# Turning the operand of the last projection earlier, and moving first logits, waits and a layer norm beside the matmuls

## The chip, the cores and the metric

One core of a Trainium2 chip runs one program. The metric is device time of one execution in microseconds; lower is better. The time before is 1919.98 us, the median of 3 runs (1919.78 to 1924.84).

## The reference

The function maps a (1, 512, 1024) f32 array through two transformer blocks, all in f32. Here is what the change touches:

```python
# first block, end of its mixer
y_attn = window_attention(q, k, v, attn_sink[l], rel_bias_table) @ w_attn_out[l]
mixed = (g_ssd * y_ssd + g_attn * y_attn) @ w_o[l]
# second block, gMLP mixer: v is (512, 2048)
v = layer_norm(jax.nn.gelu(v), ln_g, ln_b)
# second block, sliding-window attention: 16 query heads of 64, 4 key heads
logits = einsum('btkgd,bskd->bkgts', qb, kb) + alibi      # q already scaled by 1/8
m = maximum(max(logits, -1), sink); p = exp(logits - m)
o = einsum('bkgts,bskd->btkgd', p, vb) / (sum(p, -1) + exp(sink - m))
y = (o * silu(z)) @ w_out
x = x + rms_norm(y, post_g)
```

The result must hold f32 accuracy, so every large matmul is done in three passes over a high and a low part of each operand (hi*hi, hi*lo, lo*hi).

## The kernel before, in words

All engine programs are written out by hand and meet through counting semaphores; there is no planner. The 66 weight panels (1024 rows, 512 columns) stream through one buffer `raw`, `w_hi`, `w_lo` of eight tiles k. SP loads a quarter of `raw` when the low parts of the same quarter of the panel before are made (`load_quarter`, line 1045). ACT copies a tile to `w_hi` (`make_hi`, L253) once PE has finished step k of the panel before, and POOL subtracts it to get `w_lo` (`make_lo`, L257).

PE works through a panel in eight steps k (`main_step`, L294), each of 4 banks m and 3 passes, so 12 matmuls of 512 columns. Four PSUM banks `main` hold the output; the other four, `aux`, hold turned tiles, attention logits and values. The first step of a panel waits, bank by bank, until the panel before has been taken out of that bank (`bank_free`). `tail_panel` runs a panel bank by bank instead, so that rows finish one after another.

The operands of a panel that are computed in the kernel have to be turned (transposed by PE into `aux`, L366), copied to a high part (ACT, L373), and subtracted to a low part (DVE, L379). `NormOperand` counts the three as `turned`, `hi`, `ready`.

Attention (`Attention`, line 655) runs twice for each block, j = 0 and 1, 8 heads each. First comes the query panel (`query_panel`, line 1660): steps 0 to 3 for all banks, then banks 0 to 3 one at a time for the remaining steps (L1672). ACT and DVE take each finished bank as high and low queries (L713, L721). Then PE issues the logits of the first head (4 blocks c, L739 and L740; two `aux` banks in turn, so block c waits until DVE has taken block c-2), and DVE adds a bias and takes them (L780 or L782), reduces the maximum (L789), and ACT exponentiates (L806). A following panel (gates or z) has eight steps t, and in step t PE also turns the probabilities of head t-1 (L752), multiplies them with the values (L765, after ACT's copy L836) and issues the logits of head t+1. The last head, t = 7, is turned and multiplied after that panel, and by itself. ACT's tanh of z (L1494) and DVE's gating (L2114, L2116; semaphore `z_gate`) follow.

At the end of the second block all 8 tiles of the gated output `o2` are turned for the output projection P_BO, tiles 0 and 1 ahead of it, tile k+2 after step k (`turned_panel`, line 1536). The last panel is a tail panel, and the residual `res4` ends the kernel row by row (L490, L499, L521, L532, L537, L541, store L1047).

In the first block the attention output `o1` is turned one tile per step under panel P_GA+1, and `mix` for the panel P_WO: tiles 0 to 3 under P_AO+1, tiles 4 and 5 ahead of P_WO behind a wait for `ao_mul`, tiles 6 and 7 within it. DVE forms `mix` by a multiplication that frees a main bank (L2023) and an addition (L2025), bank by bank.

The gMLP's layer norm is three DVE operations on each row of 2048 columns (L2064, L2065, L2066), all before the mask of the spatial weights (L2071), which the first spatial matmul (L1749) waits for.

Of the kernel before, what the change touches and what calls it, by code (L numbers as in the profile page):

```python
# [19 lines left out]
FR = mybir.dt.float32r  # L20
# [71 lines left out]
def two_blocks(nc, d, out):  # L92
    ctx = ExitStack()
    with ctx:
# [83 lines left out]
        pt = [at("pt0", R0 + 20 * KB, [P, 384]), at("pt1", R0 + 22 * KB, [P, 384])]  # L178
        ga = at("ga", B0 + 32 * KB, [P, NT, DM])
# [291 lines left out]
        class Residual:  # L471
# [3 lines left out]
            def __init__(self, i, pan, og, gain_row, s, out_panels=2):  # L475
                self.i, self.p, self.og, self.gain_row, self.s, self.np = i, pan, og, gain_row, s, out_panels
# [4 lines left out]
            def dve_take(self, eng, n, add=False, og=None, p=None, ms=range(NT)):  # L481
                og = self.og + n if og is None else og
                p = self.p + (n + 1) * self.np - 1 if p is None else p
                for m in ms:
                    wait_full(eng, p, og, m)
                    f = fb[:, m, n * NCOL:(n + 1) * NCOL]
# [5 lines left out]
            def act_sq(self, eng, n, og=None, ms=range(NT)):  # L492
                og = self.og + n if og is None else og
                for m in ms:
# [4 lines left out]
                    eng.activation(junk_q[:, :], fb[:, m, n * NCOL:(n + 1) * NCOL], ACT.Square,  # L499
# [10 lines left out]
            def dve_gain_bank(self, eng, m, add_to=None):  # L510

                eng.wait_ge(res_sq, self.i * 2 * NT + NT + m + 1)
                eng.scalar_tensor_tensor(fb[:, m, NCOL:DM], mb[m][:, :], math.sqrt(DM), g_row[:, NCOL:DM],
                                         ALU.mult, ALU.mult).then_inc(bank_free, 1)

            def dve_gain(self, eng, ch, n, ms=range(NT)):
                eng.wait_ge(res_gain, 16 * (self.i + 1))
                for m in ms:
                    eng.wait_ge(res_sq, self.i * 2 * NT + n * NT + m + 1)
                    f = fb[:, m, n * NCOL:(n + 1) * NCOL]  # L520
# [18 lines left out]
            def dve_add_one(self, eng, m):  # L539
                eng.wait_ge(res_rs, self.i * NT + m + 1)  # L540
                eng.scalar_tensor_tensor(x_res[:, m, :], fb[:, m, :], small[:, self.s + m:self.s + m + 1], x_res[:, m, :],  # L541
# [113 lines left out]
        class Attention:  # L655
# [3 lines left out]
            def __init__(self, i, width, o, sink):  # L659
# [55 lines left out]
            def dve_take_q(self, eng, j):  # L715

                for m in range(4):
# [28 lines left out]
            def pe_turn_p(self, eng, j, t, c):  # L746
# [4 lines left out]
                for b in range(nb):  # L751
                    x = eng.transpose(self.turned_bank(t, c)[:, b * P:b * P + P], pr[t % 2][:, c, off + b * P:off + b * P + P], ident)  # L752
# [17 lines left out]
            def dve_logits(self, eng, j, t):  # L770
                for c in range(NT):
# [6 lines left out]
                    dst = lg[t % 2][:, c, off:off + nb * P]  # L778
# [7 lines left out]
            def dve_max(self, eng, ch, j, t):  # L786
                eng.wait_ge(biased, one_up(j * 32 + (self.b * 32 + t * 4 + 4)))
                mx, ng, sk = small[:, 24:28], small[:, 28 + 4 * (t % 2):32 + 4 * (t % 2)], self.sink_col(j, t)
                ch(eng.tensor_reduce(mx, lg[t % 2][:, :, 0:self.w], AX.X, ALU.max))  # L789
# [7 lines left out]
            def act_exp(self, eng, j, t, cs):  # L797
# [7 lines left out]
                for c in cs:  # L805
                    eng.activation(pr[t % 2][:, c, 0:self.w], lg[t % 2][:, c, 0:self.w], ACT.Exp,  # L806
# [49 lines left out]

            def dve_heads(self, eng, ch, j):
                self.dve_logits(eng, j, 0)
                self.dve_max(eng, ch, j, 0)
# [10 lines left out]
        att1 = Attention(0, 384, o1, "sink1")  # L870
        att2 = Attention(1, 256, o2, "sink2")
# [1389 lines left out]
```

## Time and profile before

| | before |
|---|---|
| median of 3 runs | 1919.98 us |
| profiled execution | 1920.65 us, span 1918.8 us |
| mean granted TensorE clock | 0.987 |
| PE busy | 1826.8 us (95%) |
| DVE, ACT, POOL busy | 896.3, 854.2, 862.0 us (47, 45, 45%) |
| DMA | 159.79 MB, mean 83 GB/s |
| POOL's subtraction for one `w_lo` tile (L257) | 504 times, mean 1.435 us |

The span runs from the first to the last instruction that the profile shows; the execution is 1.85 us longer. A busy engine is one with an instruction under way. An idle time of an engine is listed with its releaser, the instruction whose semaphore came last.

### The profile page before, as it was taken

To read this page: it belongs to the slowest core of one execution; us is meant where nothing else is said; L and a number is where in the kernel's file an instruction comes from. 1 tells how busy PE (TensorE), PEld (TensorE's weight loads), DVE (VectorE), ACT (ScalarE), POOL (GpSimd) and SP (SyncE) were. 2 spreads that over 40 slices of the span, in tenths; PEclk is the share of its full clock that TensorE was granted. 3 is DMA by queue.
4 is the path that set the end of the run, shared out by engine and by line. 5 is a ranking of instruction groups with operands and counts; after the bars stand their busy time and mean duration, and the time that the engine had idled before them with its cause. 6 is when DMAs were issued, how large, how long until landed. Compare 5 with 4: busy or idle time off the path is not lost.

```text
span 1918.8 us, 27606 instructions
## 1 busy us (share of the span) xinstructions
PE 1826.8 (95%) x9064; PEld 1512.2 (79%) x9064; DVE 896.3 (47%) x1311; ACT 854.2 (45%) x1796; POOL 862.0 (45%) x601
## 2 busy tenths in 40 slices
PE   8999999998999999989999999989989999999988
PEld 7787878877887878777988888867878888777766
DVE  4787888888315554234430033150261111545654
ACT  4655545554325655324442243334523332556542
POOL 4654555557353122435444444544574444531312
PEclk9999999999999999999999999999999999999989
DMA  5822211211133211422233333323222223221111
GB/s 170 145 75 67 66 55 55 65 56 55 55 110 105 72 55 50 137 77 88 88 98 99 99 92 95 109 92 128 72 93 87 88 80 108 74 83 45 55 33 56
DMA packets 46219, 159.79 MB, mean 83 GB/s; under 512 B 4763, under 2 KB 7195, under 8 KB 45884
## 3 DMA queue, kind: packets, MB, share of 16 engines
q1 hardware_dynamic: 38592, 140.53, 23.5%
q10 hardware_dynamic: 7548, 18.20, 3.8%
q8 instruction: 51, 0.84, 0.2%
q14 instruction: 28, 0.23, 0.0%
HBM read 152.42 MB, written 6.29 MB: 83 GB/s over the span
## 4 chain that ended last, share of the span: by engine, by line
PE 62%; issue 19%; DVE 9%; POOL 7%; ACT 2%; DMA 1%; DVEq 0%; ACTq 0%; POOLq 0%
PE main L294 49%; POOL w_lo L257 5%; DVE u_acc L1839 2%; PE aux L765 2%; PE main L322 2%; PE main L1672 1%; PE aux L366 1%; PE aux L1749 1%; PE aux L752 1%; PE aux L597 1%; PE aux L621 1%; DVE vv L2065 1%; DVE x_res L541 1%; PE aux L739 1%; POOL spare_lo L269 1%
## 5 line engine op out<-in xcount | busy, mean ns | idle before, releaser
L257 POOL TENSOR_TENSOR w_lo<-raw,w_hi 128x512 fp32r<-128x512 f32 x504 | 719.8, 1435 | 944.7 <-ACT w_hi L253 930.8
L253 ACT ACTIVATE w_hi<-raw 128x512 fp32r<-128x512 f32 x486 | 303.9, 630 | 700.4 <-PE main L294 687.5
L294 PE MATMUL main<-w_hi,a_hi 128*128 128x512 f32 x752 | 314.8, 419 | 2.3 <-ACT vv L1424 1.4
L294 PE MATMUL main<-w_hi,a_lo 128*128 128x512 f32 x752 | 296.9, 395 | 0.0
L294 PE MATMUL main<-w_lo,a_hi 128*128 128x512 f32 x752 | 296.0, 394 | 0.0
L294 PE MATMUL main<-a_hi,w_hi 128*128 128x512 f32 x576 | 229.6, 399 | 1.7 <-ACT u_raw L1177 1.6
L294 PE MATMUL main<-a_hi,w_lo 128*128 128x512 f32 x576 | 224.8, 390 | 0.0
L294 PE MATMUL main<-a_lo,w_hi 128*128 128x512 f32 x576 | 224.5, 390 | 0.0
L294 PEld LDWEIGHTS main<-w_hi,a_lo 128*128 128x128 f32 x752 | 142.7, 190 | 31.6
L294 PEld LDWEIGHTS main<-w_hi,a_hi 128*128 128x128 f32 x752 | 143.4, 191 | 29.7 <-issue 2.1
L294 PEld LDWEIGHTS main<-w_lo,a_hi 128*128 128x128 f32 x752 | 143.7, 191 | 23.7
L294 PE MATMUL main<-w_hi,f_hi 128*128 128x512 f32 x352 | 139.5, 396 | 6.0 <-DVE f_lo L379 6.0
L294 PE MATMUL main<-w_hi,f_lo 128*128 128x512 f32 x352 | 138.0, 392 | 0.0
L294 PE MATMUL main<-w_lo,f_hi 128*128 128x512 f32 x352 | 137.8, 391 | 0.0
L294 PEld LDWEIGHTS main<-a_hi,w_hi 128*128 128x128 f32 x576 | 108.2, 188 | 25.7 <-issue 3.0
L294 PEld LDWEIGHTS main<-a_hi,w_lo 128*128 128x128 f32 x576 | 108.1, 188 | 23.4
L294 PEld LDWEIGHTS main<-a_lo,w_hi 128*128 128x128 f32 x576 | 108.2, 188 | 22.5
L1839 DVE SCALAR_TENSOR_TENSOR u_acc<-u_raw,par,u_acc 128x510 f32<-128x510 f32 (+1 forms) x128 | 116.8, 981 | 2.4 <-DVE hst L1892 2.3
L765 PEld LDWEIGHTS aux<-v_sb,pt 128*128 128x128 f32 x544 | 70.3, 190 | 40.7 <-ACT pt L836 23.1
L765 PE MATMUL aux<-v_sb,pt 128*128 x544 | 83.7, 279 | 6.1 <-ACT pt L836 3.7
L294 PEld LDWEIGHTS main<-w_hi,f_hi 128*128 128x128 f32 x352 | 66.6, 189 | 19.6 <-DVE f_lo L379 6.2
L806 ACT ACTIVATE pr<-lg,small 128x384 f32<-128x384 f32 (+1 forms) x128 | 70.4, 552 | 24.7 <-DVE small L792 24.7
(297 smaller groups left out, 3128.9 us busy)
## 6 DMA issues: line engine op xcount, KB each, us to landing
raw<-w_stream_in SPq DMA_DIRECT2D x264, 512.0 KB, 3.5
x_res<-x_in ACTq DMA_DIRECT2D x8, 512.0 KB, 4.9
rel_rows<-rel_row ACTq DMA_DIRECT2D x1, 4096.0 KB, 44.3
bias<-rel_rows ACTq DMA_DIRECT2D x2, 1536.0 KB, 8.1
out<-x_res SPq DMA_DIRECT2D x4, 512.0 KB, 2.6
bgate<-b_gate_in ACTq DMA_DIRECT2D x4, 256.0 KB, 5.5
ln_g<-ln_g_in ACTq DMA_DIRECT2D x1, 1024.0 KB, 5.3
ln_b<-ln_b_in ACTq DMA_DIRECT2D x1, 1024.0 KB, 7.5
```

The source lines that it names most:

```text
L253: eng.activation(w_hi[:, k, :], raw[:, k, :], ACT.Copy).then_inc(hi_done, 1)
L257: eng.tensor_tensor(w_lo[:, k, :], raw[:, k, :], w_hi[:, k, :].bitcast(F32), ALU.subtract).then_inc(lo_done, 1)
L269: eng.tensor_tensor(spare.lo(k), raw[:, k, :], spare.hi(k).bitcast(F32), ALU.subtract).then_inc(lo_done, 1)
L294: mm = eng.matmul(mb[m][:, :], lhs, rhs, start=(first and k == 0 and n == 0), stop=(last and k == KT - 1 and n == 2))
L322: mm = eng.matmul(out, lhs, rhs, start=(first and k == 0 and n == 0), stop=(last and k == KT - 1 and n == 2))
L366: t = eng.transpose(b[:, m * P:m * P + P], self.src[:, m, c:c + P], ident)
L541: eng.scalar_tensor_tensor(x_res[:, m, :], fb[:, m, :], small[:, self.s + m:self.s + m + 1], x_res[:, m, :], ALU.mult, ALU.add).then_inc(r ...
L597: x = eng.matmul(ab[dr][:, :], one_row, cs_hl[:, :], start=True, stop=True)
L621: x = eng.matmul(ab[2 + i % 2][:, dr * GW:(dr + 1) * GW], b_tok[:, c, :], xw[:, dr, c, :], start=True, stop=True)
L765: x = eng.matmul(ab[3][:, c * HP:c * HP + HP], pt[c % 2][:, b * P:b * P + P], v_sb[:, lo + b, bass.ds(j * P + half * HP, HP)], start=(b == ...
L806: eng.activation(pr[t % 2][:, c, 0:self.w], lg[t % 2][:, c, 0:self.w], ACT.Exp, bias=small[:, ng + c:ng + c + 1], accum_out=small[:, sm + ...
L1839: ins = dve.scalar_tensor_tensor(acc, u_raw[:, m, i0:i0 + o1_ - o0], tap(m, k), acc, ALU.mult, ALU.add)
```

## The change

- `query_panel` calls `after(m)` behind each of its four banks. `first_logits` uses it in all four attentions: blocks 0 and 1 of the first head are issued behind bank 1, blocks 2 and 3 behind bank 2. DVE's order is that of `dve_query`.
- In block one, `o1` is turned two tiles a step in steps 0 to 3 of P_GA+1; tiles 4 and 5 of `mix` are turned behind step 1 of P_WO (with the wait for `ao_mul`), 6 and 7 behind steps 2 and 3; DVE does the four bank-freeing multiplications first and then the four additions.
- The layer norm is two operations, on 512 columns: `v_norm_cols`. The first two column blocks come before the mask, the third and fourth in the loop behind `y_lo`.
- In block two, the last head of j = 0 is issued in step 0 of the second query panel and that of j = 1 in step 0 of P_BO. Tiles 0 and 1 of `o2` are turned between steps 3 and 4 of the second query panel, 2 and 3 behind its banks 0 and 1, and 4 to 7 behind steps 2 and 3 of P_BO. The loops over j on PE, ACT and DVE are written out. Buffers: `lg2`, `pr2` (256 columns), `zt`, `fb4`, `o_hi`, `o_lo`.
- ACT makes `w_hi` tiles 0 to 2 of the last panel between its copies of the `o2` tiles 4 to 7.

```diff
+            def dve_query(self, eng, ch, j, op=None):
+                self.dve_take_q(eng, j, [0])
+                self.dve_logits(eng, j, 0, [0, 1])
+                if op is not None:
+                    op.dve(eng, [2])
+                self.dve_take_q(eng, j, [1])
+                if op is not None:
+                    op.dve(eng, [3])
+                self.dve_take_q(eng, j, [2])
+                self.dve_logits(eng, j, 0, [2, 3])
+                self.dve_max(eng, ch, j, 0)
+                self.dve_take_q(eng, j, [3])
...
+        def o_at(k):
+            return (o_hi[:, k, :], o_lo[k][:, :]) if k < 4 else (a_hi[:, k, :], a_lo[:, k, :])
+
+        op_o2 = NormOperand("op_o2", o2, [(half_k, lambda k: o_at(k)[0], lambda k: o_at(k)[1])], banks=(2, 3))
+        res4 = Residual(3, P_BO, O_BO, "b_post", 4, 1, fb4)
...
-            with act.Fori(0, 2) as j:
+            for j in range(2):
                 att2.act_take_k(act, j)
                 for k in range(4):
                     make_hi(act, j * 2 + (P_QZ + 1), k)
-                att2.act_take_q(act, j, j * 2 + P_QZ, j * 2 + O_QZ, range(3))
+                if j:
+                    op_o2.act(act, [0, 1])
+                for m in range(3):
+                    att2.act_take_q(act, j, j * 2 + P_QZ, j * 2 + O_QZ, [m])
+                    if j and m < 2:
+                        op_o2.act(act, [m + 2])
...
-            op_o2.act(act)
+            hi(P_BO + 1, [0])
+            op_o2.act(act, [4, 5])
+            hi(P_BO + 1, [1, 2])
+            op_o2.act(act, [6, 7])
             act.wait_ge(z_gate, one_up(8))
             res4.load_gain(act)
-            hi(P_BO + 1)
+            hi(P_BO + 1, range(3, KT))
...
+            def first_logits(att, j, m, og):
+                for c in {1: (0, 1), 2: (2, 3)}.get(m, ()):
+                    att.pe_logits(pe, j, 0, c, og)
...
-            panel(P_GA + 1, O_GA + 1, ao, False, aux=lambda k: op_o1.pe(pe, [k]))
+            panel(P_GA + 1, O_GA + 1, ao, False, aux=lambda k: op_o1.pe(pe, [2 * k, 2 * k + 1]) if k < 4 else None)
...
-            pe.wait_ge(ao_mul, 8)
-            op_mix.pe(pe, [4, 5])
-            panel(P_WO, O_WO, ao, False, ready=lambda k: (op_mix.ready, k + 1),
-                  aux=lambda k: op_mix.pe(pe, [k + 6]) if k < 2 else None)
+            def turn_mix_rest(k):
+                if k == 1:
+                    pe.wait_ge(ao_mul, 8)
+                    op_mix.pe(pe, [4, 5])
+                elif k in (2, 3):
+                    op_mix.pe(pe, [k + 4])
+            panel(P_WO, O_WO, ao, False, ready=lambda k: (op_mix.ready, k + 1), aux=turn_mix_rest)
...
-                        pe.wait_ge(v_norm, NT)
+                        pe.wait_ge(v_norm, j * NT + NT)
...
+            query_panel(P_QZ, O_QZ, ao, lambda m: first_logits(att2, 0, m, O_QZ))
+            heads(att2, ao, 0, P_QZ, O_QZ)
+            def turn_first_o2():
+                pe.wait_ge(z_gate, one_up(NT))
+                op_o2.pe(pe, [0, 1])
+            def under_q1(m):
+                if m < 2:
+                    op_o2.pe(pe, [m + 2])
+                first_logits(att2, 1, m, O_QZ + 2)
+            query_panel(P_QZ + 2, O_QZ + 2, ao, under_q1, under=turn_first_o2,
+                        last_head=(lambda m: att2.pe_turn_p(pe, 0, 7, m), lambda m: att2.pe_values(pe, 0, 7, m)))
+            pe.wait_ge(op_o2.ready, 4)
+            heads(att2, ao, 1, P_QZ + 2, O_QZ + 2)
+            for k in range(KT):
+                if k >= 4:
+                    pe.wait_ge(op_o2.ready, k + 1)
+                if k == 0:
+                    main_step(pe, P_BO, k, *o_at(k), False, O_BO, before=lambda m: att2.pe_turn_p(pe, 1, 7, m),
+                              after=lambda m: att2.pe_values(pe, 1, 7, m))
+                else:
+                    main_step(pe, P_BO, k, *o_at(k), False, O_BO)
+                if k == 2:
+                    pe.wait_ge(z_gate, one_up(2 * NT))
+                    op_o2.pe(pe, [4, 5])
+                elif k == 3:
+                    op_o2.pe(pe, [6, 7])
+            tail_panel(P_BO + 1, O_BO + 1, o_at)
...
+            def v_norm_cols(c0):
+                c = bass.ds(c0, NCOL)
+                for m in range(NT):
+                    part = vv[:, m, c]
+                    ch.count(dve.scalar_tensor_tensor(part, part, small[:, 16 + m:17 + m], ln_g[:, c], ALU.add, ALU.mult))
+                for m in range(NT):
+                    ch.wait(NT - 1 - m)
+                    part = vv[:, m, c]
+                    dve.scalar_tensor_tensor(part, part, small[:, 60 + m:61 + m], ln_b[:, c], ALU.mult, ALU.add).then_inc(v_norm, 1)
+            v_norm_cols(0)
+            v_norm_cols(NCOL)
...
                 y_lo(j)
+                v_norm_cols(j * NCOL + 2 * NCOL)
...
+            for j in range(2):
                 att2.dve_take_k(dve, j)
-                att2.dve_take_q(dve, j)
+                if j:
+                    op_o2.dve(dve, [0, 1])
+                att2.dve_query(dve, ch, j, op_o2 if j else None)
                 att2.dve_heads(dve, ch, j)
```

## Rows read from the trace of the kernel before

**Rows 1.** Waits of PE, whole span: waiting line, releaser, total, times, longest.
```profile
PE aux L366 <- DVE o L2116: 7.0, 1, 7.0
...
PE aux L1749 <- DVE ws_cur L2071: 5.2, 1, 5.2
PE aux L739 <- DVE lg L780: 4.9, 3, 2.2
...
PE aux L739 <- DVE lg L782: 4.5, 2, 2.2
PE aux L366 <- DVE mix L2025: 4.4, 1, 4.4
...
PE main L294 <- DVE ga L2013: 2.1, 1, 2.1
...
PE main L322 <- POOL w_lo L257: 1.8, 3, 0.7
...
PE main L294 <- DVE gt L2023: 1.1, 2, 0.7
```
**Rows 2.** Chain of work, query panel: start, us, what.
```profile
585.50 8.17 PE main L1672 x36
```
**Rows 3.** Timeline of PE, first head, block one: start, us, what, [idle before].
```profile
596.22 0.28 PE L739 MATMUL aux<-k_hh,q_hl 128*128 128x256 f32 x1
...
604.59 0.29 PE L740 MATMUL aux<-k_ll,q_hl 128*128 128x256 f32 x1
```
**Rows 4.** Timeline of PE, first head of j = 0, block two.
```profile
1714.22 0.22 PE L739 MATMUL aux<-k_hh,q_hl 128*128 128x128 f32 x1
...
1722.95 0.28 PE L740 MATMUL aux<-k_ll,q_hl 128*128 128x256 f32 x1
```
**Rows 5.** Stretches: us, busy by engine, granted clock (PEclk), DMA share, GB/s.
```profile
1712.00:1722.00 10.00, 7.76 (x33) 6.42 (x32) 6.73 (x12) 5.91 (x15) 4.97 (x4) 0.83 0.36 106
```
**Rows 6.** Timeline of DVE, first maximum of block one.
```profile
600.74 1.75 DVE L789 TENSOR_REDUCE small<-lg 128x4 f32<-128x1536 f32 x1
```
**Rows 7.** Timeline of PE, end of P_AO+1 and start of P_WO.
```profile
850.14 0.39 PE L294 MATMUL main<-w_hi,b_lo 128*128 128x512 f32 x1
...
856.59 0.77 PE L294 MATMUL main<-w_hi,a_hi 128*128 128x512 f32 x1
```
**Rows 8.** Timeline of DVE, first operation of the layer norm.
```profile
1378.77 2.31 DVE L2064 TENSOR_SCALAR vv<-vv,small 128x2048 f32<-128x2048 f32 x1 [1.13 <-POOL small L1109]
```
**Rows 9.** Timeline of DVE, residual of the last panel, beside POOL's w_lo.
```profile
1888.29 6.28 DVE L521 SCALAR_TENSOR_TENSOR fb<-fb,g_row 128x512 f32<-128x512 f32 x4 [0.66 <-ACT junk_q L499]
```
**Rows 10.** Timeline of PE, the first spatial matmuls.
```profile
1415.87 3.77 PE L1749 MATMUL aux<-vv,ws_cur 128*128 x8 [5.20 <-DVE ws_cur L2071]
```
**Rows 11.** Timeline of DVE, around the second query panel of block two.
```profile
1769.51 2.48 DVE L2109 COPY mix<-main 128x512 f32 x4 [0.25 <-DVE o L853]
...
1779.51 3.47 DVE L704 TENSOR_TENSOR k_ll<-kt_sb,k_hh 64x512 fp32r<-64x512 f32 x2
```
**Rows 12.** Timeline of PE, second last head to the last panel.
```profile
1847.22 0.50 PE L752 MATMUL aux<-const,pr 128*128 128x128 f32 x3
...
1859.98 0.79 PE L294 MATMUL main<-w_hi,a_hi 128*128 128x512 f32 x1 [0.56 <-DVE a_lo L379]
...
1864.81 0.60 PE L366 MATMUL aux<-const,o 128*128 128x128 f32 x4
1865.16 0.48 PE L294 MATMUL main<-w_hi,a_hi 128*128 128x512 f32 x1
...
1886.52 0.39 PE L294 MATMUL main<-w_hi,a_lo 128*128 128x512 f32 x1
```
**Rows 13.** Timeline of DVE, first gating operation of j = 1.
```profile
1851.73 0.69 DVE L2114 SCALAR_TENSOR_TENSOR gt<-gt,mix 128x512 f32<-128x512 f32 x1
```
**Rows 14.** Timeline of PE, values and turn within step 7, block two.
```profile
1764.70 0.60 PE L765 MATMUL aux<-v_sb,pt 128*128 x4
...
1767.96 0.66 PE L765 MATMUL aux<-v_sb,pt 128*128 x4
```

More of the change, by code:

```diff
@@ L713, in act_take_q, with dve_take_q @@
                         eng.activation(self.q_hl[half][rows, m, :], mb[m][rows, :], ACT.Copy, scale=0.125).then_inc(q_hi, 1)
-            def dve_take_q(self, eng, j):
-                for m in range(4):
+            def dve_take_q(self, eng, j, ms):
+                for m in ms:
                     for half in range(2):
@@ L768, in pe_values, with dve_logits @@
                 x.then_inc(values, 1)
-            def dve_logits(self, eng, j, t):
-                for c in range(NT):
+            def dve_logits(self, eng, j, t, cs=range(NT)):
+                for c in cs:
                     n = j * 32 + (self.b * 32 + t * 4 + c)
@@ L805, in act_exp @@
                 for c in cs:
[L806 removed]
+                    eng.activation(self.pr[t % 2][:, c, 0:self.w], self.lg[t % 2][:, c, 0:self.w], ACT.Exp,
                                    bias=small[:, ng + c:ng + c + 1],
@@ L1366, in _ @@
                     load_bgate(3)
-                    for k in range(KT):
-                        op_o1.act(act, [k])
+                    for k in range(4):
+                        op_o1.act(act, [2 * k, 2 * k + 1])
                         hi(P_AO, [k])
+                    hi(P_AO, range(4, KT))
                     act.wait_ge(op_o1.turned, KT)
@@ L1534, in head_panel @@
                         op.pe(pe, i + 4, norm)
-            def turned_panel(op, p, og, operand, feature_major, per=1, norm=None):
-                op.pe(pe, [0, 1], norm)
-                panel(p, og, operand, feature_major, ready=lambda k: (op.ready, (k + 1) * per),
-                      aux=lambda k: op.pe(pe, [k + 2]) if k + 2 < KT else None)
             pe.wait_ge(ones_set, 2)
@@ L1658, in _, with query_panel @@
                           first=(kp == 0), last=(kp == 1), k_off=8 * kp, aux=under)
-            def query_panel(p, og, operand):
+            def query_panel(p, og, operand, after, under=None, last_head=None):
                 for k in range(4):
                     h, l = operand(k)
-                    main_step(pe, p, k, h, l, True, og)
+                    if k == 0 and last_head is not None:
+                        main_step(pe, p, k, h, l, True, og, before=last_head[0], after=last_head[1])
+                    else:
+                        main_step(pe, p, k, h, l, True, og)
+                if under is not None:
+                    under()
                 for m in range(4):
@@ L1676, in query_panel, with heads @@
                             mm.then_inc(bank_full, 1)
-            def attention(att, op, j, p, og):
-                query_panel(p, og, op)
-                for c in range(NT):
-                    att.pe_logits(pe, j, 0, c, og)
+                    after(m)
+            def heads(att, op, j, p, og):
                 for t in range(KT):
```

75 lines of the change are left out of this document (35 added, 40 removed).

## Prediction, made before the changed kernel had run

> **What bounds the kernel.** I read the waits of PE first [rows 1], then PE's timeline around each long one [rows 3, 4, 7, 10, 12], then DVE's timeline there, since DVE is the releaser in nearly every line. PE is busy almost the whole span, so the end moves only by what PE stops losing: idle time before a matmul, and matmuls at the half clock behind an idle time. The reader should see in rows 1 that the eight long waits all sit where PE turns from one kind of work to the next, and that seven of them name DVE work queued at the end of a stage, while PE has matmuls that need none of it. A 512-column matmul costs 8.17 / 36 = 0.227 us [rows 2], so 12 (one step) cost 2.73 and a panel of 96 costs 21.8.
>
> **The sum, part by part, against the profiled execution (1920.65 us, span 1918.8; the median shown is 1919.98, 0.67 less).**
>
> *First logits under the query panel, block one, twice.* Before, PE needed 604.7 - 596.2 = 8.5 us from the first logits to the end of the next panel's step 0 [rows 3]: 1.2 of four logits, 2.7 of 12 matmuls, 1.2 of the four logits of head 1, and 3.4 of idle time in or behind it. After: DVE takes query 0, logits 0 and 1, query 1, query 2, logits 2 and 3, the maximum (1.75 [rows 6]), then query 3 (2 operations of 0.69, the price of 512 columns [rows 13]). Bank 3 of the query panel ends 1.2 later than before (597.4), logits 2 and 3 are taken at 597.4, maximum and its scalar end 599.5, query 3 at 600.9. PE reaches block 2 of head 1 at 600.0 and waits for DVE's first take of head 1, 601.4: a new stall of 1.4. Step 0 ends at about 602.8, 1.9 earlier. ACT's exponentials move 2 us forward with the maximum, so the following wait for the turned probabilities (about 1 us) is gone too: 2.9 each, **5.8**. Bounds: 0 (query 3 behind the maximum costs what the logits gain) to 4.4 each.
>
> *Same, block two, j = 0.* Before 1723.1 - 1714.2 = 8.9 [rows 4]; after, by the same steps with a shorter maximum, 5.7: **3.2**. In it is a fall of the clock: 0.83 granted over ten microseconds [rows 5] is 3.4 us at 1.2 GHz, at most 1.7 lost. It followed a stall of 2.2.
>
> *o1 two tiles a step.* The last tile's low part no longer stands between PE and DVE's emptying of the banks; the wait of 2.1 [rows 1] goes: **2.1**. Two tiles need 2 ACT copies and 2 DVE operations in one step of 2.73, about 2.3 in a chain; if that fails a later turn waits a few tenths. Bounds 1 to 2.3.
>
> *mix.* Under P_AO+1 the four multiplications free banks every 0.69 while PE needs one every 0.68: the two waits of 1.1 together go [rows 1], **1.1**. At P_WO, PE's last matmul was at 850.14 and the first of P_WO at 856.59 [rows 7]. After, step 0 starts at 850.4; banks are free at 849.9, 850.6, 851.2, 851.9, PE wants them at 850.4, 851.1, 851.8, 852.4. The additions end near 855.2, PE asks at 855.9. The two turns are still paid (0.7), as are all later ones; the gap gives 5.5. Nine matmuls behind it ran at twice their spacing, 1.8. **7.3**. Bounds 5 to 7.5; the additions have only 0.7 of slack.
>
> *Layer norm.* DVE begins at 1378.8 [rows 8], the first spatial matmul came at 1415.9 behind 5.2 of idle time [rows 10]. After, 16 operations of 512 columns precede the mask. An operation of this kind with both inputs in SBUF beside POOL's w_lo took 6.28 / 4 = 1.57 [rows 9], alone 0.69 [rows 13]. 16 x 1.57 = 25.1, plus 1.5 for the mask: ready at 1405.4, while PE asks at 1410.5. So the 5.2 goes, and the eight spatial matmuls that took 3.77 at the half clock cost half of that; three matmuls behind them also gain. 5.2 + 1.9 + 0.7 = **7.8**. The remaining 16 operations have over 20 us in each loop. The point at which a stall returns is 1.88 per operation; the bound at two times 1.57 gives none of the gain and costs 8 more (ends -8 and 7.9); I take 1.57, the nearest row.
>
> Rows 9 show DVE at 1.57 beside POOL against 0.69 alone, so these neighbours delay each other. The Trainium skill (SBUF — State Buffer, section Who interferes with whom) makes that speak against this edit: a DVE instruction with two SBUF inputs and a GpSimd instruction that reads SBUF exclude each other for a whole instruction, so quartered rows multiply the times that DVE can be shut out. By the rule at its worst the sum would be that of rival 2, by the row it is the one above.
>
> *Second query panel of block two.* Here the change costs. The last head is issued in step 0, which waits for DVE's copies of z (out of bank 0 at 1770.1 [rows 11]), where PE was done with head 6 at 1768.4: 1.8 idle. Step 0 with turns and values costs four times (1767.96 - 1764.70 - 0.3) / 2 = 1.5 less the first's shorter turn [rows 14], 5.4, so it ends at 1775.6. ACT's tanh queues behind the last turned block and starts at 1774.9, DVE's gating runs 1776.2 to 1782, PE wants it at 1783.8: hidden. Tiles 0 and 1: 0.7. Then DVE makes the low keys, two pairs of up to 3.47 beside POOL [rows 11], until 1788, and only then tile 0; PE wants to turn tile 2 at 1787.2: stall 1.7. Query 0 follows at 1791, logits, tile 2, query 1, tile 3, query 2, logits, maximum, query 3 at 1802: a stall of 1.0 in step 0 of the next panel, which ends at 1803.9 against 1801.4 before. The wait for probabilities of 0.7 behind it goes. With rounding: **-2.1**. Bounds -6 (keys at the worst price and a fall of the clock) to 0.
>
> *The output projection.* Before: head 6 done and the last head begun at 1847.22, first matmul 1859.98, last 1886.52 [rows 12]; end of the panel 1886.75. After, on the same origin: bank 0 free at 1849.0; step 0 with the last head to 1854.4; steps 1 and 2 to 1859.9. DVE: values out 1855, eight gating operations of 0.69 [rows 13] with one delayed by w_lo, 1861.7: a stall of 1.8. Two turns at 0.35 each (1865.16 - 1864.81 [rows 12]), step 3, two turns, steps 4 to 7: 1876.8. **9.9**. Part of it is 3 us of half clock behind the 7.0 of idle time. Bounds 6 (z later, clock falls) to 11.5.
>
> *Last panel.* w_lo of its tiles is made from step 2 on instead of after the last turn, so the 1.8 of waits goes [rows 1]: **1.8**. The residual chain of a row (5.4) fits PE's row of 5.46 as before; what follows the last matmul (8 us) is unchanged.
>
> Sum: 5.8 + 3.2 + 2.1 + 1.1 + 7.3 + 7.8 - 2.1 + 9.9 + 1.8 = 36.9. Five new stalls of 1.4 to 1.8 remain; rows 1 hold four of 2.2, of which those at 688 and 1717 were followed by a fall, and rows 5 bound one at 1.7; I subtract one fall of 1.3: **35.6**. Profiled 1885.0; median 1919.98 - 35.6 = **1884.4**.
>
> **Rivals.**
> 1. *The clock.* The short stalls that stay are enough to bring the clock down each time. For: rows 5, a fall after 2.2. Against: the same stall at 1796 left it at full speed. Price: four more falls at 1.5: 1890.5.
> 2. *DVE shut out by POOL.* Each layer norm operation waits for a whole w_lo, 1.43 in the page's mean, ahead of its own 0.69: 16 x 2.12 and 2.1 for the mask make the first spatial matmul start at 1414.8, a gain of 1 in place of 7.8; the keys and the gating around the second query panel run late by 2 more: 1893.2. For: rows 9. Against: the same rows give 1.57, not 2.12, with POOL busy throughout.
> 3. *The stalls move but do not go.* DVE's queue is in order, and in all four attentions query 3 now stands behind the maximum, the `o2` tiles behind the keys; if each place returns what it gained (18) and the clock falls behind each, as does the wait in P_BO (12), only about 5 is left: within 0.3%.
> 4. *Slower: written-out loops.* PE, ACT and DVE no longer loop over j in block two. If straight-line code could not be supplied fast enough among short instructions, each of the 128 groups (8 steps, 4 banks, 2 j, and the two query panels) would have a gap. Below 0.29 us each it only eats the gain; at 0.35 it costs 45, 1929. Against: panels P_GA to P_WO are straight-line and run at 0.227 a matmul.
>
> **How the numbers follow.** Forecast 70%, its own range 1879 to 1889; clock 11%; DVE shut out 10%; not gone 4%; slower 3%; 2% for more than the sum. A measurement of this kernel tells 0.3% (5.8 us) from nothing. The range runs from the sum without a fall and with the best ends of the panel terms, 1878, to rival 2 with two falls of the clock, 1896. Faster by over 0.3%: 0.94; within: 0.03; slower: 0.03.
>
> **What would show it.** PE's waits: no line for `o` L2116, for the mask or for `mix`; a wait at the first logits of head 1 of 1 to 1.5 in each attention; one of 1.7 before the turn of tile 2 of `o2`; one of 1.8 for `z_gate` between steps 2 and 3 of P_BO; P_BO's first matmul about 1.9 behind the last of the panel before. Granted clock over 0.99. Layer norm operations near 1.5 us. The prediction is wrong if the spatial matmul still waits over 1 us, if the second query panel loses over 5, or if instructions of PE have gaps that wait for nothing.

## The result, and the profile after

The changed kernel takes **1885.24 us** (median of 4 runs, 1884.61 to 1886.83), the kernel before 1919.95 beside it: ratio 0.9814, 95% interval 0.9802 to 0.9826. The forecast was 1884.4, range 1878 to 1896. The profiled execution took 1886.83 us, 1.8 over the sum's 1885.0 for it: span 1885.0, mean granted clock 0.986. PE is busy 1819.4 us (97%), DVE 900.7, ACT 855.2, POOL 843.0; a `w_lo` tile takes POOL 1.397 on average.

The long waits of PE in the changed kernel, over the whole span (waiting line, releaser, total, times, longest). The lines of [rows 1] have moved: L739 is now L746, L366 is L372, L1749 is L1790.

```profile
PE aux L603 <- DVE dmat L1926: 6.4, 3, 2.1
PE main L300 <- DVE f_lo L385: 6.0, 1, 6.0
...
PE aux L746 <- DVE lg L787: 3.6, 2, 1.8
...
PE aux L759 <- issue: 2.7, 2, 1.4
PE aux L772 <- ACT pt L843: 2.7, 7, 1.1
```

Of the waits of [rows 1] those on `ws_cur`, `mix`, `ga`, `gt` and `w_lo` are gone, and of the 7.0 on `o` 1.46 is left. What replaced them is short, and each stands where the prediction put it:

```profile
602.30 0.45 PE L746 MATMUL aux<-k_hh,q_hl 128*128 128x384 f32 x1 [1.81 <-DVE lg L787]
1747.78 0.30 PE L759 MATMUL aux<-const,pr2b 128*128 128x128 f32 x1 [1.36 <-issue]
1766.56 0.66 PE L372 MATMUL aux<-const,o 128*128 128x128 f32 x4 [1.66 <-DVE o_lo L385]
1780.05 0.38 PE L746 MATMUL aux<-k_hh,q_hl 128*128 128x256 f32 x1 [0.67 <-DVE lg2b L789]
1827.94 0.30 PE L759 MATMUL aux<-const,pr2b 128*128 128x128 f32 x1 [1.36 <-issue]
1840.18 1.09 PE L372 MATMUL aux<-const,o 128*128 128x128 f32 x8 [1.46 <-DVE o L2194]
```

These are lines of PE's timeline (start, duration, in brackets the idle time ahead). Predicted were 1.4, 1.8, 1.7, 1.0, 1.8 and 1.8. For the two of 1.36 the view names no releaser (`issue`). They are the wait for z's bank 0 all the same: DVE's copy out of it ends at 1827.84, PE starts at 1827.94, and with earlier copies both waits are gone (experiment 10).

Two signs that the prediction named did not come. The granted clock was to be over 0.99, and it was 0.986 in the profile and 0.989 to 0.990 in the other three runs (0.987 in the profile before). The waits at the first logits of head 1 were to be 1 to 1.5 in each attention, and they are 1.81 in block one and 0.67 in block two.

**Where the time came from.** PE issues the same matmuls of the weight panels in the same order in both kernels, so I took the same matmul in both timelines and followed how the distance of their starts grows. The whole span shrank by 33.8:

| stretch | predicted | two profiles |
|---|---|---|
| block one, first logits, both j | 5.8 | 3.0 |
| o1 two tiles a step | 2.1 | 2.6 |
| mix (under P_AO+1, at P_WO) | 1.1 + 7.3 | 9.2 |
| layer norm | 7.8 | 7.8 |
| block two, j = 0 | 3.2 | 2.6 |
| second query panel | -2.1 | -1.4 |
| output projection | 9.9 | 10.5 |
| last panel | 1.8 | 2.7 |
| clock / code that is alike in both | -1.3 | -3.2 |

The last row is four stretches that the change does not touch: at 480 (-0.6), the residual at 890 (-0.8), 1258 (-0.4) and the start of the query panel at 1670 (-1.6), with 0.2 of other drift. The clock that is granted there differs from one execution to the next with nothing changed in the code. These are windows (busy time of each engine with counts, granted clock `PEclk`, DMA share, GB/s) at 890, where the residual is made and PE turns its result, in the changed kernel and in two experiments that differ from it only elsewhere (10 and 7 below; in the second of them the same matmuls come 4.0 later, and the windows on both sides of this one are at 1.00 too):

```profile
890.00:900.00 10.00, 7.70 (x40) 7.41 (x41) 7.64 (x11) 4.29 (x11) 3.98 (x4) 0.66 0.08 23
```
```profile
890.00:900.00 10.00, 8.22 (x55) 7.93 (x56) 7.64 (x11) 4.22 (x10) 3.98 (x4) 0.83 0.10 18
```
```profile
890.00:900.00 10.00, 6.98 (x46) 5.96 (x46) 7.05 (x12) 3.92 (x11) 3.22 (x5) 1.00 0.01 2
```

In each this place begins with the same wait of PE, 1.93 or 1.94 for `a_lo`; a second one behind it is 0.8 in the first, none in the second and 1.1 in the third, so PE's idle time does not order them. Both others are 1.5 us shorter here than the first. So where such a place lies inside a stretch, a single profile tells the stretch to about 1.5 us only.

### The profile page after: what moved, and what is told of

It reads as the page before. It is cut to its first block, busy times and chain, and to the rows that moved or that the text cites. A ratio compares the mean times of both kernels' runs of the same rounds, so it can differ in the third digit from the quotient of the medians.

```text
span 1885.0 us, 27143 instructions
## 1 busy us (share of the span) xinstructions
PE 1819.4 (97%) x9064; PEld 1511.0 (80%) x9064; DVE 900.7 (48%) x1331; ACT 855.2 (45%) x1795; POOL 843.0 (45%) x601
## 4 chain that ended last, share of the span: by engine, by line
PE 80%; DVE 8%; issue 6%; ACT 3%; POOL 1%; DVEq 0%; ACTq 0%; POOLq 0%
PE main L300 61%; PE main L328 4%; PE aux L772 3%; PE main L1702 2%; PE aux L759 1%; DVE u_acc L1904 1%; PE aux L746 1%; PE aux L372 1%; PE aux L603 1%; DVE x_res L547 1%; PE aux L627 1%; PE aux L747 1%; PE aux L636 1%; PE aux L1790 1%; DVE small L796 1%
## 5 line engine op out<-in xcount | busy, mean ns | idle before, releaser
L263 POOL TENSOR_TENSOR w_lo<-raw,w_hi 128x512 fp32r<-128x512 f32 x504 | 700.8, 1397 | 926.4 <-ACT w_hi L259 911.7
L300 PE MATMUL main<-w_hi,a_hi 128*128 128x512 f32 x736 | 306.4, 416 | 1.7 <-ACT vv L1447 1.4
L300 PE MATMUL main<-w_hi,a_lo 128*128 128x512 f32 x736 | 289.8, 394 | 0.0
L300 PE MATMUL main<-w_lo,a_hi 128*128 128x512 f32 x736 | 289.1, 393 | 0.0
L772 PEld LDWEIGHTS aux<-v_sb,pt 128*128 128x128 f32 x544 | 70.8, 191 | 39.3 <-ACT pt L843 24.1
L772 PE MATMUL aux<-v_sb,pt 128*128 (+1 forms) x544 | 83.5, 279 | 4.3 <-ACT pt L843 2.7
L843 ACT ACTIVATE pt<-aux 128x256 f32<-128x256 f32 (+2 forms) x128 | 50.7, 397 | 63.9 <-PE aux L759 60.9
```

The source lines that it names most:

```text
L263: eng.tensor_tensor(w_lo[:, k, :], raw[:, k, :], w_hi[:, k, :].bitcast(F32), ALU.subtract).then_inc(lo_done, 1)
L300: mm = eng.matmul(mb[m][:, :], lhs, rhs, start=(first and k == 0 and n == 0), stop=(last and k == KT - 1 and n == 2))
L772: x = eng.matmul(ab[3][:, c * HP:c * HP + HP], pt[c % 2][:, b * P:b * P + P], v_sb[:, lo + b, bass.ds(j * P + half * HP, HP)], start=(b == ...
L843: eng.activation(pt[c % 2][:, 0:nb * P], self.turned_bank(t, c)[:, 0:nb * P], ACT.Copy).then_inc(p_in, 1)
```

## The experiments

All are the changed kernel with one thing different, except the third, which is the kernel before with one thing done. "By stretch" is how much the distance of the same matmuls, against the changed kernel's profile, grows over the stretch that the experiment touches. Medians are set against the changed kernel's 1885.2 in its own runs, and 1886.0 in the last set of four. The kernel before took 1919.73 beside experiments 1 to 4, 1920.90 beside 5 to 8 and 1921.14 beside 9 to 12, so medians of different sets compare to about 1 us.

**1. The layer norm of before.**

```diff
-            v_norm_cols(0)
-            v_norm_cols(NCOL)
+            for m in range(NT):
+                row = vv[:, m, :]
+                ch(dve.tensor_scalar(row, row, small[:, 16 + m:17 + m], small[:, 60 + m:61 + m], ALU.add, ALU.mult))
+                ch(dve.tensor_tensor(row, row, ln_g[:, :], ALU.mult))
+                dve.tensor_tensor(row, row, ln_b[:, :], ALU.add).then_inc(v_norm, 1)
```

> The changed kernel with the layer norm of before (three operations on 2048 columns per row, all ahead of the mask), nothing else undone. Theory (each part's gain stands by itself, as the sum had it): the wait of 5.2 before the first spatial matmul comes back with the half-clock matmuls behind it, so about 7.8 us more than the changed kernel: 1893.0. Rival (gains of one stage are partly given back in a later one, so parts overlap): less than 4 more, under 1889.

Measured 1893.06 (1891.01 to 1893.16), 7.8 more; by stretch 7.9. PE's only wait in 1300 to 1440 is the old one:

```profile
PE aux L1790 <- DVE ws_cur L2139: 5.2, 1, 5.2
```

The gain of the layer norm stands by itself, to a tenth of its term.

**2. The mix of before.**

```diff
-                for m in range(NT):
-                    c = slice(n * NCOL, (n + 1) * NCOL)
                     dve.wait_ge(bank_free, 4 * (O_AO + n) + m + 1)
...
+            pe.wait_ge(ao_mul, 8)
+            op_mix.pe(pe, [4, 5])
```

> The changed kernel with the mix of before: multiplication and addition bank by bank, tiles 4 and 5 turned ahead of P_WO behind the wait for ao_mul. Theory: the waits of 4.4 + 1.1 and the half-clock matmuls come back: the sum said 8.4, the matmuls of the two profiles stand 9.2 apart over this stretch, so 1893.6 to 1894.4. Rival (the wait is the only cost, the clock not): 5.5 more, 1890.7.

Measured 1896.15 (1893.07 to 1898.16). The profiled execution is the lowest of the four, 8.9 by stretch; the median says 10.9. The two waits are back, and behind the long one the half clock, which the rival left out:

```profile
PE aux L372 <- DVE mix L2090: 4.4, 1, 4.4
...
PE main L300 <- DVE gt L2088: 1.1, 2, 0.7
```
```profile
850.00:860.00 10.00, 10.00 (x43) 8.41 (x43) 2.08 (x3) 2.13 (x4) 0.00 (x0) 0.76 0.09 36
```

**3. The kernel before, with the loops over j of block two written out.**

```diff
-            with pe.Fori(0, 2) as j:
+            for j in range(2):
                 attention(att2, ao, j, j * 2 + P_QZ, j * 2 + O_QZ)
```

> The kernel before with only one thing done: the loops over j of block two written out on PE, ACT and DVE. Theory (instruction supply is no limit): 1920.0, within 1 us of the kernel before. Rival (straight-line code is supplied too slowly at the groups of short instructions): 5 us or more slower, and idle times of PE that wait for nothing in 1690 to 1850. Third: leaving the loops saves their turn-over, 1 to 2 us faster.

Measured 1919.61 (10 runs, 1918.42 to 1921.09), ratio 0.9997 with an interval of 0.9987 to 1.0006. Straight-line code costs nothing here, and leaving the loops gives nothing that can be measured. Rival 4 falls.

**4. The first logits of block one behind the query panel again.**

```diff
-                query_panel(p, og, op, lambda m: first_logits(att, j, m, og))
+                query_panel(p, og, op, lambda m: None)
+                for c in range(NT):
+                    att.pe_logits(pe, j, 0, c, og)
...
+                att1.dve_take_q(dve, j, range(4))
                 dve.wait_ge(bias_landed, j * 16 + 16)
-                att1.dve_query(dve, ch, j)
+                att1.dve_logits(dve, j, 0)
+                att1.dve_max(dve, ch, j, 0)
```

> The changed kernel with the first logits of block one (both j) behind the query panel again and DVE's old order there; block two stays changed. Theory as predicted: 2 x 2.9 = 5.8 more, 1891.0. Rival, from laying the two profiles side by side (2.1 at j = 0, 0.9 at j = 1, since a stall of 1.8 stays in each and the half clock at 690 falls on more matmuls): 3.0 more, 1888.2.

Measured 1887.13 (1886.14 to 1890.83), 1.9 more; the intervals (0.9816 to 0.9849 against 0.9802 to 0.9826) overlap. By stretch it is 2.9, 2.1 at j = 0 and 0.9 at j = 1, which is the rival's figure. In its profile 1.2 of that is hidden by the clock at 480, in code that is alike (0.98 granted there, 0.86 in the changed kernel's profile). The edit swapped a wait of 2.2 for one of 1.8. Here are the old waits, from 580 to 800:

```profile
PE aux L746 <- DVE lg L787: 4.4, 2, 2.2
PE aux L772 <- ACT pt L843: 1.7, 6, 0.4
```

**5. Whole rows in the two-operation layer norm.**

```diff
-                c = bass.ds(c0, NCOL)
+                c = slice(0, DI)
...
-            v_norm_cols(NCOL)
...
-                v_norm_cols(j * NCOL + 2 * NCOL)
```

> The changed kernel, but the two layer norm operations take whole rows of 2048 columns, all 8 ahead of the mask. Theory A (beside POOL's queue of w_lo each DVE operation is held up for about one fixed time, whatever its length: the profile of before has 3.26 for 2048 columns with two full inputs, 0.5 over 4 x 0.69, that of the changed kernel 6.86 / 4 = 1.72 for 512, 1.03 over 0.69): 8 x 3.27 = 26.2 us from 1365.4, mask at 1391.6, PE asks at 1398.4, no wait, 1885.2, as with half of the rows' columns. Theory B (a price per column, two to two and a half times the lone one): 8 x 6.3 = 50, mask at 1416, a wait of 18, 1903.

**6. POOL quiet beside the layer norm.** Most of the 16 `w_lo` tiles is left out. It was run once, for its profile.

```diff
+            for p in (P_UZ + 1, P_UZ + 2):
+                for k in range(KT):
+                    pool.wait_ge(hi_done, p * 8 + k + 1)
+                    pool.tensor_tensor(w_lo[:, k, 0:32], raw[:, k, 0:32], w_hi[:, k, 0:32].bitcast(F32),
+                                       ALU.subtract).then_inc(lo_done, 1)
```

> The changed kernel, with POOL's subtraction for the 16 w_lo tiles of panels P_UZ+1 and P_UZ+2 cut to 32 of 512 columns (so most of these w_lo is left out). Theory (the layer norm's 1.2 to 1.7 per operation is POOL's w_lo beside it): 16 operations at 0.69 to 0.75, done some 11 to 12 us after the first in place of 24.1, and the same total, since PE did not wait there: 1885. Rival (the operation with two full inputs and a scalar costs that by itself, or ACT or the DMA slows it): over 1.2 still.

These two belong together. DVE's timeline of the changed kernel, then of the quiet one (groups of 4 operations with their total):

```profile
1365.44 6.86 DVE L2135 SCALAR_TENSOR_TENSOR vv<-vv,small,ln_g 128x512 f32<-128x512 f32 x4 [1.13 <-POOL small L1131]
1372.22 6.88 DVE L2139 SCALAR_TENSOR_TENSOR vv<-vv,small,ln_b 128x512 f32<-128x512 f32 x4
1379.02 5.84 DVE L2135 SCALAR_TENSOR_TENSOR vv<-vv,small,ln_g 128x512 f32<-128x512 f32 x4
1384.79 4.80 DVE L2139 SCALAR_TENSOR_TENSOR vv<-vv,small,ln_b 128x512 f32<-128x512 f32 x4
1389.51 0.41 DVE L2147 TENSOR_TENSOR ws_cur<-wsT,const 128x256 f32<-128x256 f32 x1
```
```profile
1363.05 2.74 DVE L2140 SCALAR_TENSOR_TENSOR vv<-vv,small,ln_g 128x512 f32<-128x512 f32 x4 [1.13 <-POOL small L1131]
...
1373.66 0.41 DVE L2152 TENSOR_TENSOR ws_cur<-wsT,const 128x256 f32<-128x256 f32 x1
```

The 16 operations take 24.1 us beside POOL and 10.6 without (1363.05 to 1373.7). The total of experiment 6 is 1884.9, as PE did not wait for them in either.

The means by four (1.2 to 1.7) hide what happens. Operation by operation there are only two durations. These are the first norm operation and POOL's tiles of the same time in the changed kernel (shortest, median and longest in ns), then the norm operation of the quiet kernel:

```profile
L2135 DVE SCALAR_TENSOR_TENSOR vv<-vv,small,ln_g x8: 741/1774/1781, 1365.4 to 1384.1; 128x512 f32<-128x512 f32 x8
L263 POOL TENSOR_TENSOR w_lo<-raw,w_hi x10: 1736/1741/1748, 1366.6 to 1381.9; 128x512 fp32r<-128x512 f32 x10
```
```profile
L2140 DVE SCALAR_TENSOR_TENSOR vv<-vv,small,ln_g x8: 735/740/751, 1363.0 to 1370.3; 128x512 f32<-128x512 f32 x8
```

While POOL has tiles, the two engines take turns, one operation for one tile, a pair every 1.70 us. Of the 16 operations 13 take 1.77 or 1.78; the other three, once POOL has to wait for ACT's `w_hi`, take 0.74 as in the quiet kernel. So the price is set by how many operations there are, as long as POOL has work. With whole rows, DVE and then POOL (its eight tiles beside these operations), ACT and PE read:

```profile
1365.85 13.26 DVE L2135 SCALAR_TENSOR_TENSOR vv<-vv,small,ln_g 128x2048 f32<-128x2048 f32 x4 [1.13 <-POOL small L1131]
...
1392.22 1.51 DVE L2146 TENSOR_TENSOR ws_cur<-wsT,const 128x256 f32<-128x256 f32 x1
```
```profile
L263 POOL TENSOR_TENSOR w_lo<-raw,w_hi x8: 3327/3336/3339, 1367.0 to 1390.1; 128x512 fp32r<-128x512 f32 x8
```
```profile
1394.11 0.63 ACT L259 ACTIVATE w_hi<-raw 128x512 fp32r<-128x512 f32 x1 [4.07 <-DMA raw<-w_stream_in]
...
1396.05 2.07 ACT L1471 ACTIVATE sz<-main 128x512 f32<-128x512 f32 x4
```
```profile
1396.70 0.50 PE L300 MATMUL main<-w_hi,a_hi 128*128 128x512 f32 x1 [1.89 <-ACT sz L1471]
```

DVE's part went as theory A said: 13.26 / 4 = 3.3 for four times the columns, so the mask (1393.7) is in time. But its profile is by stretch 3.6 longer, and the median is 1888.22 (1885.28 to 1890.87), though its interval (0.9810 to 0.9842) overlaps that of the changed kernel. What neither theory had is the other side. It is still one operation for one tile, and now each of POOL's tiles beside the long operations takes 3.34, where it took 1.74 beside the short ones and takes 1.3 alone. Its `w_lo` frees `raw` late, the load lands late, ACT's `w_hi` waits for it 4.07, and ACT's emptying of the main banks queues behind that. PE waits 1.89 for it, and 0.90 and 0.93 of the clock are granted in the two windows of ten microseconds from 1390 on, where the changed kernel has 1.00. Short operations are dear for DVE and cheap for POOL; the change picked the form that the stage can bear.

The Trainium skill (SBUF — State Buffer, section Who interferes with whom) says that of a DVE instruction with two SBUF inputs and a GpSimd instruction that reads SBUF, one blocks for the whole length of the other. The traces agree that the two take turns by whole instructions: 1.77 against 0.74 for DVE with POOL on and off, 3.34 against 1.74 for POOL with DVE's operations long and short. They don't show a full exclusion: a pair every 1.70 is less than the 0.66 and 1.25 us from start to start that the two need alone (DVE in experiment 6, POOL at 596 to 601).

**7. o1 one tile a step.** ACT's copies of the turned tiles follow the same order.

```diff
-panel(P_GA + 1, O_GA + 1, ao, False, aux=lambda k: op_o1.pe(pe, [2 * k, 2 * k + 1]) if k < 4 else None)
+panel(P_GA + 1, O_GA + 1, ao, False, aux=lambda k: op_o1.pe(pe, [k]))
```

> The changed kernel with op_o1 turned one tile a step under all eight steps of P_GA+1, as before. Theory as predicted: the wait for ga (2.1) at the start of P_AO comes back, 2.1 more: 1887.3; the two profiles say 2.5. Rival (the pairs only moved the wait, and P_GA+1 pays for them): no change, 1885.2.

Measured 1889.63 (1887.55 to 1890.31), 3.6 to 4.4 more than the changed kernel's two medians; by stretch 4.0. That is over the theory. The wait returns as it said, with a fall of the clock behind it that the kernel before did not have in its profile:

```profile
PE main L300 <- DVE ga L2077: 2.1, 1, 2.1
```
```profile
800.00:810.00 10.00, 9.94 (x37) 8.15 (x38) 1.70 (x3) 5.37 (x10) 3.04 (x3) 0.83 0.61 245
```

**8. The last head of j = 1 by itself, ahead of P_BO.**

```diff
+            att2.pe_turn_p(pe, 1, 7, 0)
+            for c in range(NT):
+                if c < 3:
+                    att2.pe_turn_p(pe, 1, 7, c + 1)
+                att2.pe_values(pe, 1, 7, c)
             for k in range(KT):
...
-                if k == 0:
-                    main_step(pe, P_BO, k, *o_at(k), False, O_BO, before=lambda m: att2.pe_turn_p(pe, 1, 7, m),
-                              after=lambda m: att2.pe_values(pe, 1, 7, m))
-                else:
+                if True:
                     main_step(pe, P_BO, k, *o_at(k), False, O_BO)
```

> The changed kernel with the last head of j = 1 issued by itself ahead of P_BO, as before, while tiles 0 to 3 are still turned early and 4 to 7 behind steps 2 and 3 of P_BO. It parts the gain of 9.9 in the output projection. Theory A (most of the gain is that PE has steps 0 to 2 to do while tanh and gating run; interleaving the head saves the chain of turn, copy and values, four times about 1, less the 1.4 that step 0 then waits for z's bank): 2 to 3.5 more, 1887.2 to 1888.7. Theory B (the head's place is what counts, since z's gate is released by it): the wait for z_gate grows by as much as the head takes, 6 or more.

A miss of both theories, in sign: 1883.12 (1881.08 to 1885.13), **less** than the changed kernel. The intervals (0.9787 to 0.9820 against 0.9802 to 0.9826) overlap, so the medians alone don't prove it; by stretch it is 2.6 less, from 1829 to 1842, where both profiles are granted 1.00. Here are PE and DVE of the changed kernel, with head 6's last values, step 0 (its turn at 1827.94 behind 1.36 idle is shown above) and the release of the gate:

```profile
1825.92 0.66 PE L772 MATMUL aux<-v_sb,pt 128*128 128x64 f32 x4
...
1827.99 0.48 PE L300 MATMUL main<-w_hi,o_hi 128*128 128x512 f32 x1
```
```profile
1833.29 0.42 DVE L860 TENSOR_TENSOR o<-aux,small 128x256 f32<-128x256 f32 x1 [3.38 <-PE aux L772]
```

and of this experiment:

```profile
1825.91 0.50 PE L759 MATMUL aux<-const,pr2b 128*128 128x128 f32 x3
...
1827.80 1.28 PE L772 MATMUL aux<-v_sb,pt 128*128 128x64 f32 x8
1828.89 0.48 PE L300 MATMUL main<-w_hi,o_hi 128*128 128x512 f32 x1
...
1837.18 1.03 PE L372 MATMUL aux<-const,o 128*128 128x128 f32 x8
```
```profile
1829.44 0.42 DVE L860 TENSOR_TENSOR o<-aux,small 128x256 f32<-128x256 f32 x1
```

The head alone takes 3.0 us, half of it in the time in which step 0 otherwise waits for z's bank; interleaved, its last values come at the end of step 0, so DVE's output and the gating start at 1833.29 against 1829.44, which is 3.4 later when counted from head 6's output (1826.69 and 1826.18), and PE waits 1.46 at the turn of tiles 4 and 5, where it now does not wait at all.

**9. Logits of head 1 ahead of query 3.**

```diff
                 self.dve_max(eng, ch, j, 0)
+                self.dve_logits(eng, j, 1, [0])
                 self.dve_take_q(eng, j, [3])
...
-                        self.dve_logits(eng, j, t + 1)
+                        self.dve_logits(eng, j, t + 1, range(NT) if t else (1, 2, 3))
```

> The changed kernel with one order changed on DVE, in all four attentions: it takes logits block 0 of head 1 right behind the maximum of head 0, and query 3 only then. Theory (the stall of 1.81 at block 2 of head 1 in block one, 0.67 in block two, is DVE's query 3, 1.4 us, standing ahead of that take): the waits L746 <- lg of 3.6 and 1.3 go, 4.9 us, and some matmuls of half clock at 690 with them: 1880 to 1880.5. Rival (query 3 is late then, and PE waits for bank 3 of the main banks instead, or the exponentials hold the next step): under 2 gained.

Measured 1882.43 (1881.15 to 1883.80), 3.6 less than the 1886.04 of its set. By stretch it is 2.1 less in block one (0.5 at j = 0 and 1.6 at j = 1) and 0.4 less in block two, where 1.3 of waits went and a wait of 0.6 for bank 3 and 0.4 more for turned probabilities came; about 1.1 more of its profile's gain lies at 480, in code that is alike. Between the two expectations: the wait is gone, and part of the rival came true, in block one as a wait of 0.8 each for bank 3. At j = 1 the clock no longer falls behind the wait. Here are this experiment's wait, its window, and that of the changed kernel:

```profile
PE main L300 <- DVE q_hl1a L728: 1.6, 2, 0.8
```
```profile
690.00:700.00 10.00, 9.83 (x64) 7.95 (x63) 5.99 (x11) 5.45 (x15) 2.22 (x2) 1.00 0.11 27
```
```profile
690.00:700.00 10.00, 10.00 (x54) 8.52 (x55) 4.98 (x10) 5.66 (x18) 1.28 (x1) 0.83 0.18 52
```

**10. Three orders in block two.**

```diff
-                att2.dve_take_k(dve, j)
+                att2.dve_take_k(dve, j, [0])
                 if j:
                     op_o2.dve(dve, [0, 1])
+                att2.dve_take_k(dve, j, [1])
...
-                att2.dve_heads(dve, ch, j)
...
+                att2.dve_heads(dve, ch, j, lambda: take_z(range(3)))
+                take_z([3])
...
+                        if (k, m) == (3, 1):
+                            pe.wait_ge(z_gate, one_up(2 * NT))
+                            op_o2.pe(pe, [4, 5])
+                        elif (k, m) == (4, 3):
+                            op_o2.pe(pe, [6, 7])
```

> The changed kernel with three orders changed in block two: DVE copies z banks 0 to 2 ahead of the output of head 6; it makes the low parts of o2 tiles 0 and 1 between the two halves of the low keys; PE turns tiles 4 and 5 in the middle of step 3 of P_BO, 6 and 7 behind step 4. Theory: the waits of 1.36 twice (turn of the last head), 1.66 (tile 2) and 1.46 (z_gate) go, and about 0.3 comes back for tile 4's low part: 5.6 less, 1879.6. Rival (the copies of z ahead hold up the output of head 6, whose bank the last head's values need; each wait returns in the next one): under 2 gained.

Measured 1879.89 (1878.52 to 1880.75), 6.2 less. The three orders were changed in one run, but the stretches part them: 1.5 less at each of the two turns of a last head (1749 and 1829), 1.9 at tile 2 (1768), 1.4 in the output projection. PE's waits from 1690 to the end of its profile, as the view lists them, are these:

```profile
PE aux L772 <- ACT pt L843: 1.4, 3, 1.1
PE aux L746 <- DVE lg2b L789: 1.3, 2, 0.7
```

**11. The last two together.**

> Both of the last two together. Theory (the waits are independent): 10.5 less than the changed kernel, 1874.7. Rival (fewer short stalls, or a fall of the clock somewhere else, take part of it back): 1878 to 1880.

Measured **1876.22** (1875.21 to 1876.90), ratio 0.9767 with an interval of 0.9751 to 0.9783: 9.8 less than the changed kernel, 44.9 less than the kernel before beside it. That is the sum of the two gains (3.6 and 6.2), so the waits are independent, nothing is given back, and this version beats both kernels.

**12. The changed kernel again.**

> The changed kernel itself, on the same chip as the three before it, as what they are compared with: 1885.2, and the same waits as in its first profile; the granted clock between 880 and 1260 and between 1640 and 1680 may differ by a few tenths in single windows, up to 2 us in the span.

Measured 1886.04 (1885.06 to 1887.19), ratio 0.9818, interval 0.9802 to 0.9835. Its waits are as before; the windows at 1640 and 1650 hold 0.66 and 1.00 where the first profile had 0.84 and 1.00.

## Why the prediction was right, point by point

**The first logits of block one were mis-sized**, the one term that was clearly off: 5.8 predicted (2.9 at each j), 3.0 by the two profiles (2.1 and 0.9), 2.9 by experiment 4. The mechanism was right (the stall moves to head 1 and stays), its length was not: 1.81 for 1.4. DVE's timeline of the changed kernel:

```profile
597.51 1.75 DVE L796 TENSOR_REDUCE small<-lg 128x4 f32<-128x1536 f32 x1
599.42 0.94 DVE L799 TENSOR_SCALAR small<-small,par 128x4 f32<-128x4 f32 x1 [0.16 <-DVE small L796]
600.40 0.69 DVE L728 SCALAR_TENSOR_TENSOR q_hl<-main,q_hl 64x512 fp32r<-64x512 f32 x1
601.10 0.69 DVE L728 SCALAR_TENSOR_TENSOR q_hl1a<-main,q_hl1a 64x512 fp32r<-64x512 f32 x1
601.82 0.89 DVE L787 TENSOR_TENSOR lg<-aux,bias 128x256 f32<-128x256 f32 x2
```

Query 3 was put at 599.5 and began at 600.4, and PE went on at 602.3 in place of 601.4. Most of this 0.9 is the scalar behind the maximum, which took 0.94, where the median of its 32 operations is 0.23. That is the 0.8 by which j = 0 fell short of its 2.9. At j = 1 the clock took 1.2 more, which the sum did not have. A window of 0.83 follows the new wait at 690 as one followed the old wait at 688, but before, it cost nothing: the waits behind it, 0.52 and 0.99 at j = 0, shrank to none and 0.23 at j = 1, and both j took the same 29.4 us from bank 3 of the query panel to step 3 of the next one. In the changed kernel the first steps behind the new wait have only 0.17 of waiting left for it to hide in. The lower bound (0) held the value. Experiment 9 bears this out: with the take ahead of query 3 the wait of 1.81 goes, and 2.1 us come, most of them at j = 1 where the clock stays at 1.00.

**o1 two tiles a step**: 2.1 predicted, 2.6 by the profiles, 3.6 to 4.4 by experiment 7. The wait is as priced. The upper bound of 2.3 was too tight; it left out that the clock can fall behind the wait.

**mix**: 8.4 predicted, 9.2 and 8.9 by stretch, no wait left. **Layer norm**: 7.8 in all three. Its price of 1.57 an operation was 24.1 / 16 = 1.51, the mask took 0.41 in place of 1.5, so it was ready at 1389.9, and PE asked at 1397.2. The price was near for a reason that the sum did not have: 1.51 is a mean of thirteen operations held up by one tile each and three that were not. That is the mechanism of rival 2 (each operation waits for a whole `w_lo`), with 1.70 a pair in place of 2.12. Rival 2 fell on the price. At 1.70 for all 16 the mask would have been ready at 1393, still in time.

**Block two, j = 0**: 3.2 and 2.6. **Second query panel**: -2.1 and -1.4 (its own steps, 1803.9 - 1801.4 less 0.7, add up to -1.8, not -2.1); its stalls of 1.8 and 1.7 were 1.36 and 1.66, and the one of 1.0 was 0.67.

**Output projection**: 9.9 and 10.5. From head 6 done, the turn of tiles 4 and 5 was predicted at 14.5 and came at 13.6, the panel's end at 29.6 and 29.1. The sum was right, but one belief behind it was not: that the last head in step 0 is part of the gain. It costs 2.6 (experiment 8). The rest of the edit, early turns of tiles 0 to 3 and three steps that PE does while the gating runs, then gives some 13 (10.5 + 2.6, a sum; no run took it away by itself). The prediction had the head's output ("values out 1855") ahead of the gating, but it did not price the other order, in which that output comes earlier.

**Last panel**: 1.8 and 2.7. **The clock**: I subtracted 1.3 for a fall behind a new stall. Only one came behind a new stall (690), and the old kernel had one at the same place; the 3.2 us of the last row lie in unchanged stretches and come and go with the execution. In the median of the runs, 34.7 less than before, the error of the sum is 0.9. Part of this is luck: the terms' errors are -2.8, +0.5, +0.8, 0, -0.6, +0.7, +0.6, +0.9, and cancel to 0.1; the clock's is -1.9 in the profiled execution, the slowest of the four.

**Rival 1** (four more falls at 1.5 behind the new stalls) did not come, **rival 3** neither: of its 18 us some 3 returned, the 2.8 that the first logits fell short. **Rival 4** was tried by itself (experiment 3) and costs nothing.

What stays open: why the same place at 890 is granted 0.66 in some executions and 1.00 in others; and whether the last head ahead of P_BO adds to the version of experiment 11, whose earlier copies of z take part of the same wait. That pair was not run.

## What to carry to other kernels

When a helper engine's queue is in order, price a moved operation by what it pushes back: here two 0.69 us operations ahead of one take held back 2.5 us of what the early logits can gain, by the stretches of experiment 9 (3.6 by its medians). Interleaving a piece of work with matmuls is free only if nobody waits for its result; the last head, which releases a chain of tanh and gating, is better issued at once. DVE and POOL took turns here, one instruction for one. So short DVE operations beside POOL cost DVE more than double (1.77 for 0.74) and POOL a third (1.74 for 1.3), and long ones cost DVE little and POOL more than double (3.34 for 1.3): choose the length by which of the two has slack. And look at single durations: a mean of four hid the two values.

## What the runs showed of the hardware that was not expected

An operation on 4 columns can be held up nearly as long as one on 512: the scalar behind the maximum took up to 0.97 us with POOL's `w_lo` beside it, 0.23 in the median of 32. These are its group, and POOL's tile that was under way when the one at 599.42 began:

```profile
L799 DVE TENSOR_SCALAR small<-small,par x32: 228/230/974, 599.4 to 1822.8; 128x4 f32<-128x4 f32 x32
```
```profile
599.04 1.30 POOL L263 TENSOR_TENSOR w_lo<-raw,w_hi 128x512 fp32r<-128x512 f32 x1
```

The tile ends at 600.34 and the scalar 0.03 later. The other two that took 0.95 or more (at 686.94 and 1702.23) end in the same way 0.02 behind the tile that was under way when they began. So the trace has it wait for the tile to end; only the layer norm's operations were also run with POOL quiet. And the granted clock at one and the same place, begun with the same wait of PE, was 0.66, 0.83 or 1.00; the first profile took 1.5 us longer there than either other.
